# Late adaLN vectors multiplied inside the first mixer steps, and attention values with v as the stationary operand

## The reference, cut to what matters

```python
mod = silu(c) @ w_ada + b_ada            # c: one row per sequence; w_ada: 1024 x 6144
sh1, sc1, g1, sh2, sc2, g2 = split(mod, 6)
h = x * (1 + sc1) + sh1                  # needed first, for every token
proj = h @ w_in                          # 1024 x 1792: q, k, v, a, g
attn = softmax_with_sink(q k^T + bias, window of 128 + own chunk) @ v   # 8 heads of 64, 2 kv heads
mix  = concat(attn, conv) @ w_out        # 1024 x 1024
x    = layer_norm(ALPHA * x + (1 + g1) * mix)     # g1, then sh2 and sc2, are needed later
h2   = x * (1 + sc2) + sh2               # then a mixture of experts; g2 after it
```

## Time and profile before

| | |
|---|---|
| time, median of 3 runs | 1598.95 us (1598.3 to 1603.15) |
| the profiled execution's own time, its span | 1604.14 us, 1601.5 us |
| busy share: PE, DVE, ACT, POOL | 85%, 79%, 50%, 40% |
| `setup` | 0 to about 123.8 us |
| `mix`: first turn of x; one full step | at 135.2 us; 42.9 us |

### The profile page before, as it was taken

One profiled execution on the slowest core, in us unless ns is written; L12 is line 12 of the kernel. 1 busy time (PEld: TensorE's weight loads), 2 busy tenths in 40 slices (PEclk: granted clock), 3 DMA queues, 4 the chain that ended last, 5 costly groups with the idle time before them and its releaser, 6 DMA issues. The chain is left out here.

```text
span 1601.5 us, 23606 instructions
## 1 busy us (share of the span) xinstructions
PE 1353.3 (85%) x7116; PEld 727.4 (45%) x7116; DVE 1258.6 (79%) x3143; ACT 794.6 (50%) x1447; POOL 645.2 (40%) x487
## 2 busy tenths in 40 slices
PE   5995889999999999999996514999999999996664
PEld 1113555555555555555554203445444444443221
DVE  0520999999999999999997146999999999994588
ACT  0410334444444444444443202889889888884122
POOL 0002337666766666776444430222222222220753
PEclk9997999999999999999996755999999999998798
DMA  9963102111111111111111157477895233222997
GB/s 317 395 243 142 49 1 80 54 54 54 53 45 37 52 42 53 53 41 54 40 45 40 40 201 251 165 250 260 296 388 199 105 109 114 114 108 99 240 330 243
DMA packets 90724, 218.47 MB, mean 136 GB/s; under 512 B 8035, under 2 KB 42759, under 8 KB 88592
## 3 DMA queue, kind: packets, MB, share of 16 engines
q1 hardware_dynamic: 65554, 136.25, 23.8%
q0 software_dynamic: 11808, 43.00, 9.2%
q10 hardware_dynamic: 13277, 38.20, 6.2%
HBM read 165.90 MB, written 51.56 MB: 136 GB/s over the span
## 5 line engine op out<-in xcount | busy, mean ns | idle before, releaser
L1015 DVE SCALAR_TENSOR_TENSOR y_sum<-uT,w_dw_cols,y_sum 128x128 f32<-128x128 f32 (+1 forms) x1804 | 467.9, 344 | 0.0
L1755 DVE SCALAR_TENSOR_TENSOR w_gate_up_lo<-w_gate_up_ring,w_gate_up_hi 128x2048 f16<-128x2048 f16 x96 | 219.4, 2287 | 37.0 <-ACT w_gate_up_hi L1677 36.9
L1677 ACT ACTIVATE w_gate_up_hi<-w_gate_up_ring 128x2048 f16 x96 | 182.8, 1906 | 59.2 <-SPq L1635 39.5
L1153 PE MATMUL bank<-w_in_hi,hT_hi 128*128 128x512 f16 (+3 forms) x544 | 194.7, 358 | 13.3 <-ACT v L849 11.6
L1658 POOL COPY slot_index<-slot_token 128x1 int32 (+1 forms) x48 | 57.7, 1201 | 352.4 <-PE eturn L1819 309.7
L1153 PE MATMUL bank<-w_in_lo,hT_hi 128*128 128x512 f16 (+3 forms) x544 | 194.7, 358 | 0.0
L1153 PE MATMUL bank<-w_in_hi,hT_lo 128*128 128x512 f16 (+3 forms) x544 | 194.4, 357 | 0.0
L1798 PE MATMUL ps_up<-w_gate_up_hi,slot_rowsT_hi 128*128 128x512 f16 x384 | 147.0, 383 | 24.2 <-DVE slot_rowsT_lo L1780 24.0
L1798 PE MATMUL ps_up<-w_gate_up_lo,slot_rowsT_hi 128*128 128x512 f16 x384 | 146.6, 382 | 0.0
L1798 PE MATMUL ps_up<-w_gate_up_hi,slot_rowsT_lo 128*128 128x512 f16 x384 | 146.5, 382 | 0.0
L1786 DVE SCALAR_TENSOR_TENSOR w_down_lo<-w_down_ring,w_down_hi 128x2048 f16<-128x2048 f16 x48 | 109.7, 2285 | 5.9 <-ACT w_down_hi L1731 5.7
(11 more groups left out here) (265 smaller groups left out, 2924.6 us busy)
## 6 DMA issues: line engine op xcount, KB each, us to landing
w_ada_ring<-in_w_ada SPq DMA_DIRECT2D x12, 2048.0 KB, 15.1
expert_rows<-out_rows ACTq DMA_DIRECT2D x48, 512.0 KB, 2.7
w_gate_up_ring<-in_w_gate SPq DMA_DIRECT2D x16, 1024.0 KB, 8.5
w_gate_up_ring<-in_w_up SPq DMA_DIRECT2D x16, 1024.0 KB, 11.4
w_down_ring<-in_w_down SPq DMA_DIRECT2D x16, 1024.0 KB, 12.5
x_h<-in_x_prompt SPq DMA_DIRECT2D x16, 512.0 KB
x_res<-in_x_prompt SPq DMA_DIRECT2D x16, 512.0 KB, 3.5
hidden<-h SPq DMA_DIRECT2D x16, 512.0 KB, 2.6
```

Of the source, the lines that this page charges most:

```text
L1015: dve.scalar_tensor_tensor(total, u, w, y_sum[:, c, :n], ALU.mult, ALU.add).then_inc(taps_done, 1)
L1153: mm = pe.matmul(out, x[xp][:, k, :n], w[wp][:, k, cols], start=(k == 0 and wp == xp), stop=(k == KD - 1 and xp == 1))
L1677: act.activation(gate_up_parts[0][:, at, k:k + KD // 2, :, :].rearrange("p k a n -> p (k a n)"), w_gate_up[:, bass.ds(b, 1), k:k + KD // 2 ...
L1755: dve.scalar_tensor_tensor(flat[1], w_gate_up[:, bass.ds(b, 1), k, :, :].rearrange("p b k a n -> p (b k a n)"), W_SCALE, flat[0], ALU.mult ...
```

## The change

`setup` now multiplies only sh1 and sc1, in 8 chunks of 256 columns. The stationary operand is silu(c) repeated over 64 columns for each sequence, so the product is already the broadcast rows for 64 sample and 64 prompt partitions; DVE adds the bias rows and writes `rows[:, 0:2]` directly. POOL modulates tile 0 in `setup`. ACT begins with w_in at once; w_out is loaded by SP into the ring's buffers when these are done with, with its rows regrouped for the new order of heads. At its end SP loads the bias and norm rows of the four later vectors in twelve DMAs of 256-byte runs.

`mix` multiplies the four later vectors in 16 products of 256 columns, two in each of eight slots: step 0 after kv and after the turn of x, steps 1 and 2 after kv, after the router's place, and after the turn of x. A product has four column tiles of 32 with 64 moving columns each, in the score banks. DVE adds them into `rows[:, 4]`; SP stores the finished vectors to DRAM in eight small DMAs each and reads them back as broadcast rows. Their w_ada chunks come through a ring of two buffers.

The values product gets v as stationary operand (64 columns, two column tiles for the two kv heads) and the turned probabilities as 128 moving columns, so its output is already turned. PE spreads 1/den over partitions by eight matmuls in the place of the turn of o; ACT copies that; DVE multiplies in the next step, ACT makes the upper half and POOL the remainder.

```diff
+ADA_COLS = 256
+ADA_SLOTS = {"scores": {0: 0, 1: 2, 2: 5}, "router": {1: 3, 2: 6}, "turned": {0: 1, 1: 4, 2: 7}}
 # setup, SP (after the eight small loads of pack)
+                for h in range(2):
+                    load_ada(h)
...
+                for k in range(KD):
+                    if k % 2 == 0 and k < 6:
+                        sp.wait_ge(ada_done, ADA_FIRST - 2 + k // 2)
+                    if k >= 6:
+                        sp.wait_ge(hi_ready, KD + k - 6 + 1)
+                        sp.wait_ge(lo_ready, KD + k - 6 + 1)
...
+                    if k == 3:
+                        sp.wait_ge(mod_ready, ADA_FIRST)
+                        sp.dma_start(vec_rows[0:2, 0, :], M["rows"][SMP:SMP + 1, 0:2, :]).then_inc(vec_stored, 16)
+                for b in range(4):
...
+                sp.wait_ge(later_loaded, 16 * 12)
 # setup, ACT: pieces among the small work instead of behind it
+                for i in range(3):
+                    top(i)
...
+                top(3)
                 act.wait_ge(bias_stored, 16)
...
+                for i in range(4, 6):
+                    top(i)
 # setup, PE
+                for h in range(ADA_FIRST):
+                    pe.wait_ge(ada_loaded[h % ADA_RING], 16 * (h // ADA_RING + 1))
+                    if h >= 2:
+                        pe.wait_ge(mod_ready, h - 1)
                     for k in range(KD):
+                        mm = pe.matmul(ps_mod[h % 2][:, 0:ADA_COLS], c_tiled[:, k, :], w_ada[h % ADA_RING][:, k, :], start=(k == 0), stop=(k == KD - 1))
+                    if h == 2:
                         turn_small()
 # setup, DVE
+                for h in range(ADA_FIRST):
+                    rest(h)
+                    v, q = divmod(h, ADA_QUARTERS)
+                    dve.wait_ge(ada_done, h + 1)
+                    part = M["rows"][:, 1 - v, q * ADA_COLS:(q + 1) * ADA_COLS]
+                    dve.scalar_tensor_tensor(part, ps_mod[h % 2][:, 0:ADA_COLS], 1.0 * v, part, ALU.add, ALU.add).then_inc(mod_ready, 1)
+                for i in range(ADA_FIRST, len(pieces)):
+                    rest(i)
 # mix, SP
+                def load_ada(h):
+                    if h >= 2:
+                        sp.wait_ge(ada_used, h - 1)
+                    sp.dma_start(w_ada[h % 2], ada_v[:, :, ada_columns(*ADA_LATER[h])]).then_inc(ada_loaded[h % 2], 16)
...
+                    if is_tile(i, 1):
+                        for h in range(6, 12):
+                            load_ada(h)
+                        sp.wait_ge(row_steps, 1)
+                        store_row(2, 0)
...
+                    if is_tile(i, 2):
+                        sp.wait_ge(row_steps, 5)
+                        store_row(5, 3)
+                        sp.wait_ge(mod_stored, 16 * 8 * 4)
+                        for v in range(3, 5):
+                            sp.dma_start(rows[:, v, :], row(v, 1)).then_inc(rows_loaded, 16)
 # mix, POOL
+                        pool.wait_ge(oT_hi_ready, count(1, j, 1))
+                        pool.tensor_tensor(mixT[1][:, 0:4, :n], o_norm[:, :, :n], mixT[0][:, 0:4, :n], ALU.subtract).then_inc(oT_ready, 1)
 # mix, ACT: after y_tok, and at the end of a step
+                        act.wait_ge(o_ready, count(1, j, 1))
+                        act.copy(mixT[0][:, 0:4, :n], o_norm[:, :, :n]).then_inc(oT_hi_ready, 1)
...
-                        for h in range(HEADS):
-                            cols = slice(h * HD, (h + 1) * HD)
-                            last = act.activation(o_tok[:n, cols], OB["pv"][:n, cols], ACT.Copy, scale=rden[:n, KV * (h % GROUP) + h // GROUP:KV * (h % GROUP) + h // GROUP + 1])
-                        last.then_inc(o_ready, 1)
+                        act.copy(o_norm[:, :, :n], turn_bank("r", 0)[:, :, :n]).then_inc(r_copied, 1)
 # mix, DVE: use of a product; o is multiplied where the remainder was made
+                    dve.wait_ge(ada_done, h + 1)
+                    part = acc[:, v - 2, q]
+                    dve.scalar_tensor_tensor(part, score[h % 2][:, 0, 0:ADA_BLOCK], 0.0 if v == 3 else 1.0, part, ALU.add, ALU.add).then_inc(ada_used, 1)
...
+                        dve.tensor_tensor(o_norm[:, :, :n], OB["pv"][:].rearrange("p (g q) -> p g q", g=GROUP)[:, :, :n], o_norm[:, :, :n],
+                                          ALU.mult).then_inc(o_ready, 1)
 # mix, PE
+                def ada_product(h):
+                    pe.wait_ge(ada_loaded[h % 2], 16 * (h // 2 + 1))
+                    if h >= 2:
+                        pe.wait_ge(ada_used, h - 1)
+                    for k in range(KD):
+                        for b in range(4):
+                            mm = pe.matmul(score[h % 2][32 * b:32 * b + 32, 0, 0:ADA_BLOCK], silu[:, k, :],
+                                           w_ada[h % 2][:, k, b * ADA_BLOCK:(b + 1) * ADA_BLOCK], start=(k == 0), stop=(k == KD - 1))
+                    mm.then_inc(ada_done, 1)
...
+                    if (j := lagged(i, 1)) is not None:
+                        pe.wait_ge(scores_used, count(4, j, 2 if place == "scores" else 4))
...
+                        ada_emptied(i, "scores")      # waits ada_used before score rounds 2 and 3
...
-                                    mm = pe.matmul(OB["pv"][:n, h * HD:(h + 1) * HD], pT[:nk, f % 2, e, kt, :n], v,
+                                    mm = pe.matmul(OB["pv"][s * HD:(s + 1) * HD, f * P:f * P + n], v, pT[:nk, f % 2, s, kt, :n],
...
-                        turn_in(i, "o", 0, [(c, o_tok[:n, c * P:(c + 1) * P], n, P) for c in range(4)], o_turned)
+                        for g in range(GROUP):
+                            for s in range(KV):
+                                x = KV * g + s
+                                mm = pe.matmul(turn_bank("r", 0)[s * HD:(s + 1) * HD, g, :n], rden[:n, x:x + 1].to_broadcast([n, HD]),
+                                               ident[:n, :n], start=True, stop=True)
```

More of the change, by code:

```diff
@@ L181, in build @@
             }
+            M["x_h"] = held("x_h", [P, 2, D])
+            M["rows"] = held("rows", [P, 5, D])
+            M["x_res"] = held("x_res", [P, D])
+            M["late"] = held("late", [P, 4, D])
             setup(nc, a, K, M, vec_rows, bias_rows)
@@ L535, in mix @@
         u_out = sb("u_out", [P, CH])
-        v1 = sb("v1", [P, D])
-        n1 = sb("n1", [P, D])
-        h2 = sb("h2", [P, D])
-        h2T = sb("h2T", [P, KD, P])
+        v1, n1, h2 = (M["late"][:, n, :] for n in range(3))
+        h2T = M["late"][:, 3, :].rearrange("p (k t) -> p k t", k=KD)
+        w_ada, ada_v = ada_ring(M), ada_view(a)
+        acc, norm, silu = later_tiles(M)
         part_logits = sb("part_logits", [P, P])
@@ L561, in mix @@
         h2_stored = sem("h2_stored")
+        ada_loaded = [sem(f"later_ada_loaded{n}") for n in range(2)]
+        mod_stored = sem("mod_stored")
         n1_stored = sem("n1_stored")
         cache_stored = {n: sem(f"cache_stored_{n}") for n in ("sample", "prompt")}
+        ada_done = sem("later_ada_done")
         x_turned = sem("x_turned")
@@ L1097, in step @@
                         taps(j1, cuts[3], cuts[4])
+                    use_slot(i, "router")
                     if j1 is not None:
@@ L1233, in step @@
                         mm.then_inc(logits_done, 1)
+                    ada_slot(i, "router")
                     if j1 is not None:
```

284 lines of the change are left out of this document (162 added, 122 removed).

## The result

The changed kernel takes 1561.66 us (median of 4 runs, 1560.28 to 1561.93) against 1599.45 for the kernel before, a ratio of 0.975 with a 95% interval of 0.973 to 0.977. Forecast were 1559 us and a range of 1538 to 1581. The profiled execution before was a long one (1604.14 us, 4.7 above the median), so the stages add up to some 4 us more than the 37.8 between the medians.

What follows compares the result with a forecast made beforehand. DMA was taken to bound setup's start, with PE idle before the first turn of x, and PE to bound full steps. 1604.1 - 61 + 25 - 4 = 1564 us profiled, 1559 by the median; range 1538 to 1581.

Steps and rivals of the forecast that it cites:

- Setup, -61 forecast: Setup: first turn of x at 74 us instead of 135.2, with PE's products no longer setting the end; -61 us.
- DVE's tail is eight remainders of 1.17: End of setup: DVE's remainders of w_out run from 60 us, when the vectors are ready, to 69.5.
- lie beside it: End of setup: POOL's two-operation modulation of the sample tile, 60 to 65 us, was to add nothing to setup's end.
- The first rival: Setup ends late: twelve short-run DMAs come last at w_router's rate; first turn at 88 us, total 1573 us; chance 0.15.
- Steps 0 to 2, +25 forecast: First three mixer steps: sixteen products cost 18.5 us in eight slots, plus changed waits; +25 us, bounds +12 and +40.
- The second rival: Later products: a record has a floor near 25 ns, so slots cost 8.5 us more; 1568 us; chance 0.09.
- the added and dropped waits: Steps 0 to 2: new PE waits of 2, 4, 2 and 1 us, with 3.2 us of old waits gone.
- Values, -0.3 a step forecast: Full step: values stretch 5.78 to 4.95 us, spread of 1/den +0.7, copies give back 0.16; -4 us over 15 tiles.
- The cover named in the prediction: Full step: POOL's new 1.15 us falls ahead of the next tile's modulation, with 1.5 us of slack remaining.
- Column tiles one after another: Products and values: tiles do not overlap, a record costs 0.11 us; 1694 us, slower; chance 0.04.
- the third rival: Steps 1 and 2: PE's present waits hide half of the added 25 us, values gain 14; 1537 us; chance 0.12.
- The fifth rival: Full step: copies of the probabilities set the values stretch, so it stays at 42.9 us; 1563 us; no own chance.

Runs made afterwards that it cites:

- the run with POOL late: Changed kernel, but POOL's modulation of the sample tile in setup waits until DVE has done all remainders of w_out; 1565.03 us in one run.
- another kernel: Changed kernel with setup reordered: two pieces of w_out in free slots of w_in's ring, nine short-run DMAs between the large loads; 1561.36 us.
- the modulation part alone: Changed kernel with values product, output scalings and turn of o put back as before; 1564.66 us, ratio 0.977 to the kernel before.
- 896 records less: Changed kernel with each of the sixteen later products doing only the first of its eight k blocks; 1555.23 us in one run.

## Why the prediction was right

The time and the sign came out: 1564 us for the profiled execution against 1561.93. Each term had its mechanism, but three were mis-sized. Setup gave 5.9 less than forecast and steps 0 to 2 cost 6.5 less, and step 17's 4.8, which stood in no term, makes up for what the values and step 18 lacked. That the total fits to some 2 us is therefore luck in good part.

**Setup, -61 forecast, -55.1 measured.** PE does not set the end, as forecast, and the eighth piece of w_in came at 55.4 (57 forecast). Two terms were short. The vectors were put at 60, though the terms named for it (57 + 1.7 + 2.0 + 0.4) add up to 61.1, and came at 65.4: the seventh chunk of w_ada landed only at 55.6, and the last two products took 9.34 instead of 7.0, the first 4.4 us of it at the lower level. And "DVE's tail is eight remainders of 1.17" took 13.5 us instead of 9.4: two of the remainders took 3.4 us beside POOL's modulation, said to "lie beside it", which excludes DVE for its whole length. Of this 4.1 some 2 would have been lost anyway, to late pieces of w_out, as the run with POOL late shows. SP's last DMA of w_out waits for the second remainder, done at 69.8, so the short-run DMAs began at 70.25 where the forecast has 63. Without that lock, with one remainder taken ahead of the vectors and with a shorter tail of DMAs the turn of x comes at 76.6, inside the forecast's 68 to 80; the changed kernel's own 80.16 lies just outside. The price of the twelve short-run DMAs was about right at the end of an emptying queue: 8.7 us from the first issue to the last landing against the 9 forecast, and they end setup together with DVE. The first rival's price, read from a full queue, did not come; in such a queue another kernel had single issues of 3 us and a rate of 109 GB/s.

**Steps 0 to 2, +25 forecast, +18.5 measured.** The slots cost 8 x 1.92 = 15.4, not 18.5: 15 ns a record, with hardly anything for going in and out. The second rival's floor of 25 ns is not there. In "TensorE: Matmul & The Clock Gate" (section "Wait — 56ns, not 53.3ns?") the Trainium skill states it for the distance from one matmul's start to the next; here matmuls that go to different column tiles start 6 to 7 ns apart, so for these the trace does not agree. Records in one tile stand 56 ns apart. PE's idle time grew by 6.2 (from 10.8 to 17.0), where the added and dropped waits made 5.8. Single waits were off: the turn of z waits 6.53 and not 5.75, chunks of w_ada held PE for 2.1 in all and not 2 a slot. PE's busy time grew by 12.3, less than the slots' 15.4: the lower clock held 17 us instead of 20, and part of the values' gain lies here. With the modulation part alone these steps grew by 23.5, near the forecast, at the lower clock for 32 us; the rest of the difference came, in these executions, with the new values. A clock that the change itself moves had no term in the sum.

**Values, -0.3 a step forecast, -0.12 measured.** The stretch (4.95 forecast, 5.01 measured) and the spread (1.11 and 1.02) came out, -0.77 and +0.58; what was to come back behind the copies of the output did not. The 4.95 is less sure than it looks: the terms named for it (1.33, four blocks of 0.43, two turns of 0.44, a wait of 0.4) add up to 4.33, and to 5.33 with 0.25 a block for going in and out; a block took 0.59. So fourteen steps gave 1.7 us instead of 4. Step 17's 4.8 us, which hide this in the total, go with the clock; the kernel without the new values has them too.

**Step 18, not priced, +1.8.** POOL's new remainder was costed at nothing because 1.5 us of slack cover it in a full step. In step 18 no modulation follows and the out product waits for it; moving it ahead of x1 took 2.4 us off. Where DVE makes that remainder (the modulation part alone), the out product stands 22.25 us behind the turn of y, as in the kernel before (22.10), against 23.63 in the changed kernel. The cover named in the prediction holds only in steps that have it.

**Rivals.** Column tiles one after another cost 57 ns a record, close to the 55 from which that rival was to decide; the time was 1596.75 and not 1694, since the forecast of the price, 0.11 from a values record with 128 stationary columns instead of 32, was twice too high and the values were left alone in that run. That the steps hide half of the added time (the third rival) was wrong: they grew by 18.5, and PE's idle time there grew too. The fifth rival (full steps of 42.9, 1563 us) lies nearer to the 42.76 and 1561.66 measured than its chance suggests, but not by its reason: the stretch that the copies were to set became 0.77 us shorter.

## What to carry to other kernels

Price a moved piece of work in the first and last steps of a pipeline too, not only in the full one: what covers it there may be missing. Where four column tiles share PE, alternate them matmul by matmul; two matmuls in a row for one of two tiles cost nothing here, eight in a row for one of four cost three times the time. Before a few us in a stretch with gaps on PE are put down to an edit, compare the granted clock of the same stretch in both kernels.

## What was not expected of the hardware

- DVE's remainders (1.17 us, two inputs in SBUF) and POOL's modulation (2.33) exclude each other operation by operation: 3.2 us each where they meet. In a full step DVE's taps did not wait: in the changed kernel 20 of them ran in 5.25 us beside an operation of POOL's that took its usual 2.35. The taps read one of their two tensors, y_sum, from PSUM:

```profile
304.78 5.25 DVE L1094 SCALAR_TENSOR_TENSOR y_sum<-uT,w_dw_cols,y_sum 128x128 f32<-128x128 f32 x20
...
304.88 2.35 POOL L880 TENSOR_TENSOR late<-late,rows 128x1024 f32<-128x1024 f32 x1
```

  So they are not operations with two inputs in SBUF; that this spares them was not tried.
- 896 records less gave 5.3 us instead of 13 in one execution, in which PE ran more of its work at 1.2 GHz.
- The same 148 PE instructions of step 17 took 43.94 us at a granted clock of 0.65 and 38.13 at 0.78.
- Four column tiles of float32 matmuls with 64 columns run 3.7 times as fast as one; in the order tile by tile 1.2 times. Tile by tile, and with the values in the other order, a record started ahead of three that were issued before it for another tile.
